# Attention of a fused transformer kernel: context keys laid in front of the tokens, and output halves joined by transposes and a sum

## The chip, the cores and the metric

The kernel runs on one core of a Trainium2 chip. The metric is device time in microseconds (us) of one execution; the runs shown are of the unchanged kernel. Engines: TensorE (PE; its weight loads are PEld), VectorE (DVE), ScalarE (ACT), GpSimd (POOL), and SyncE (SP), which issues the transfers. PSUM holds eight banks of 512 fp32 columns by 128 partitions; here three tensors S of two banks and two tensors M of one bank.

## The reference, cut to what matters

The program computes two transformer blocks over 1024 tokens of width 1024. The first has an attention with two kinds of heads, both of width 64, and 256 context keys that every query sees beside its local ones; the second block (a gated linear attention) and both feed-forward parts are not touched. What is computed in the attention:

```python
# kind a: 8 query heads, 2 key heads, window of 128 to either side, one sink per head
s_loc = einsum('bnqkgd,bnjkd->bnkgqj', qb, kb) * scale      # up to 384 local keys
s_loc = where(mask, s_loc, -inf)
s_ctx = einsum('bnqkgd,bjkd->bnkgqj', qb, k_ctx) * scale    # 256 context keys
p = softmax(concatenate([s_loc, s_ctx, sink_col], -1), -1)
o = einsum('bnkgqj,bnjkd->bnqkgd', p_loc, vb) + einsum('bnkgqj,bjkd->bnqkgd', p_ctx, v_ctx)
# kind b: 8 heads, 2-D neighbourhood of 8 x 16 positions, bias by offset, no sink
s_loc = einsum('bnqhd,bnjhd->bnhqj', qb, kg) * scale + bias # 512 or 576 local keys
...
```

Softmax is over the concatenation, so the order of the keys is free as long as scores and values agree.

## The kernel before, in words

All five engines run their own straight program, written out by Python loops; the order on each is that of the code, and signals (semaphores) tie them. The phases are: the input norm and the product with the input weights, in 18 units (`UNITS`, kinds k, q and v), attention, output product, feed-forward, second block, feed-forward. In each product, fp32 values are split into a high and a low fp32r part, and three of the four part products are summed.

A k unit gives 128 rows (two heads of 64) by 1280 columns: before, columns 0 to 1023 are tokens and 1024 to 1279 context keys, in `ka`, `kb`, and in their split copies `kh` and `kl`. TensorE has the token part in an S tensor and the context part in an M tensor; VectorE takes both out (`unit_take`), ScalarE and TensorE form the norm (`unit_norm`, `unit_sums`), and the a keys are rotated (`unit_rope`).

Attention is one software pipeline over 128 items `ITEMS`: 16 heads, 8 blocks of 128 queries each, the first 64 of kind a, the last 64 of kind b. L is the number of local keys: 256 or 384 for a, 512 or 576 for b. In iteration i the engines do, in this order:

- TensorE: `join(i-4)` (L520, L521), `scores(i)` (L551, L552, and the mask products L554 of kind a), `turn_weights(i-1)` (L567, a transpose for each 128 keys), `weigh(i-2)` (L583).
- VectorE: `take_out(i-4)` (L1317), the minimum of the negated scores (L1341 and L1345 for a; L1347 and L1351 with the bias for b), the low part of the weights of item i-1 (L1362); in every second iteration of the b part also half a row of the modulation product (L1373).
- ScalarE: the high part of the weights of item i-1 (L928), exp of item i (L935), the copy `ot` of the weighed values of item i-2 (L941).
- GpSimd: the division by the sums, and the split of the next head's queries, keys and values; SyncE moves their halves to the other partitions.

Scores of item i lie in `S[i % 2]`, columns 0 to 255 + L, at most 832; the joined output of item i lies in the same S tensor at columns 960 to 1023. `ot` has 128 partitions (64 dimensions of v's high part, then 64 of its low part) and 256 columns (128 queries by the weights' high part, then by their low part). The join multiplies both column halves with `ii`, an identity stacked twice, in plain fp32, so that queries come to lie on partitions and all four parts are summed in PSUM; in the trace each such product is two instructions (x2). VectorE then copies 64 columns out. It does this after the scores of item i+4, which TensorE issues behind the join into the same S tensor:

```python
e.wait_ge(*scored(i + 4))
e.tensor_copy((oa if kind == "a" else ob)[:, b, 64 * h:64 * h + 64], S[i % 2][:, 960:1024])
```

Scores are written as column pieces, each a product with `kh` and one with `kl`: context (256 columns), first 256 tokens, the rest.

Of the kernel before, what the change touches and what calls it, by code (L numbers as in the profile page):

```python
# [13 lines left out]
KB = 1024  # L14
# [182 lines left out]
def build(nc, T, out):  # L197
    o = 16512

    def at(name, off, shape, dt):  # L200
        return nc.alloc_sbuf_tensor_at(name, shape, dt, offset=off)
# [57 lines left out]
    osq = at("osq", AH + 37 * KB, [128, 512], F)  # L259
    ii = at("ii", AH + 39 * KB, [128, 64], F)  # L260
    ot = at("ot", AH + 61 * KB, [128, 2, 256], F)
# [35 lines left out]
    def flat(x):  # L297
        return x.rearrange("p a b -> p (a b)")

    def vo_part(m):  # L300
# [4 lines left out]
    with ExitStack() as ctx:  # L305
# [39 lines left out]

        SL, ML, BANK = Slots(3), Slots(2), {}

        def unit_tile(u):
# [7 lines left out]
        def tensor_program(e):  # L356
# [82 lines left out]
            def unit_sums(u):  # L439
# [15 lines left out]
                e.wait_ge(*a_sq(u))  # L455
                e.matmul(S[j][:, 0:512], blk, sq[:, 0:512], start=True, stop=True)
                i = e.matmul(S[j][:, 512:1024], blk, sq[:, 512:1024], start=True, stop=True)
                if kind == "k":
                    i = e.matmul(M[jc][:, 0:256], blk, sq[:, 1024:1280], start=True, stop=True)
                i.then_inc(*summed.mark(u))  # L460

            def unit_rope(u):
                kind, m, rope = UNITS[u]
                if not rope:
                    return
                dst = ka[:, :] if kind == "k" else qa[:, m, :]
# [48 lines left out]
            def join(i):  # L515
                s = i % 2
                e.wait_ge(*a_ot(i))
                if i == 0:
                    e.wait_ge(*d_set("ii"))
                e.matmul(S[s][:, 960:1024], ot[:, i % 2, 0:128], ii[:, :], start=True, stop=False)  # L520
                e.matmul(S[s][:, 960:1024], ot[:, i % 2, 128:256], ii[:, :], start=False, stop=True).then_inc(*joined.mark(i))  # L521

            def scores(i):
# [17 lines left out]
                D, Q = S[s], qs[:, z, 128 * b:128 * b + 128]  # L541
                w, n1 = 256 + L, min(256, L)
                parts = [(0, 256, 1024, None)]
                if kind == "a":
                    parts.append((256, 256 + n1, k0, (256, mlb) if b > 0 else (384, mrb)))
                    if L > 256:
                        parts.append((512, w, k0 + 256, (512, mrb)))
                else:
                    parts += [(256, 512, k0, None), (512, w, k0 + 256, None)]
                for c0, c1, kc, m in parts:  # L550
                    e.matmul(D[:, c0:c1], Q, kh[:, z, kc:kc + c1 - c0], start=True, stop=False)  # L551
                    i_ = e.matmul(D[:, c0:c1], Q, kl[:, z, kc:kc + c1 - c0], start=False, stop=m is None)  # L552
                    if m is not None:
                        i_ = e.matmul(D[:, m[0]:m[0] + 128], idb[:, :], m[1][:, :], start=False, stop=True)  # L554
# [235 lines left out]
        def scalar_program(e):  # L790
# [44 lines left out]
            def unit_norm(u):  # L835
                kind, m, rope = UNITS[u]
                j = SL.of["sum", u]
                if kind == "v":
# [4 lines left out]
                    return  # L843
                dst, w = unit_tile(u)
                e.wait_ge(*d_ev(u))
                if u > 0:
# [6 lines left out]
                if u > 0:  # L853
                    e.wait_ge(*d_nrm(max(v for v in range(u) if UNITS[v][0] != "v")))
                i = e.activation(rs[:, 0:1024], S[j][:, :], ACT.Ln, bias=EPS)
                i.then_inc(*a_ln.mark(u))
                last = u
                if kind == "k":
                    last = ("c", u)
                    e.activation(rs[:, 1024:1280], M[ML.of["sum", u]][:, 0:256], ACT.Ln, bias=EPS).then_inc(*a_ln.mark(last))  # L860
                e.wait_ge(*a_ln(last))
# [337 lines left out]
        def vector_program(e):  # L1199
# [46 lines left out]
            def unit_take(u):  # L1246
# [10 lines left out]
                else:  # L1257
                    d = unit_tile(u)[0]
                if kind != "q":
                    e.tensor_copy(d[:, 1024:1280], M[ML.of[u]][:, 0:256]).then_inc(*d_ev.mark(("c", u)))  # L1260
                e.tensor_copy(d[:, 0:1024], S[SL.of[u]][:, :]).then_inc(*d_ev.mark(u))

# [38 lines left out]
            e.wait_ge(*summed(NU - 1))  # L1301
            e.tensor_tensor(ii[:, :], cst[:, C_ID:C_ID + 64], cst[:, C_ID + 64:C_ID + 128], ALU.add).then_inc(*d_set.mark("ii"))
            e.memset(pp[:, :, 832:896], 0.0).then_inc(*d_set.mark("pad"))
# [7 lines left out]
            def take_out(i):  # L1311
# [267 lines left out]
        def gpsimd_program(e):  # L1579
# [20 lines left out]
            def unit_rope(u):  # L1600
                kind, m, rope = UNITS[u]
                if not rope:
                    return
                x = unit_tile(u)[0][:, 0:1024]
                e.wait_ge(*roped(u))
# [458 lines left out]
```

## Time and profile before

| | |
|---|---|
| median of 3 runs | 2894.28 us (2889.22 to 2894.30) |
| profiled execution | 2890.93 us, its span 2889.1 us |
| mean granted TensorE clock | 0.975 of full speed |
| busy share of the span | TensorE 94%, its weight loads 77%, VectorE 34%, ScalarE 34%, GpSimd 32% |
| attention: L1317, first and last start | 404.3 and 769.6 us |

The shares are those of the whole span; most of it is long products, in which TensorE alone sets the pace. In the attention stage the other engines have much higher shares, so it is read by itself. In a row of the timeline the first number is the start, the second the duration; where a row merges several instructions the duration is from the first start to the last end, and a bracket says how long the engine had been idle and what ended that.

### The profile page before, as it was taken

The page shows a single profiled execution, that of the slowest core. Times are in us where ns is not written, and L with a number is a line of the kernel's source. Part 1 is how long each engine was busy: PE and PEld are TensorE (multiplying, and loading weights), DVE is VectorE, ACT ScalarE, POOL GpSimd, SP SyncE. Part 2 cuts the span into 40 slices and gives each one's busy share as a digit, 9 for nine tenths or more (in the row PEclk, how much of TensorE's full clock was granted, in tenths as well). Part 3 has the DMA queues.
Part 4 walks back from the last instruction along what each step waited for, and adds up shares of the span by engine and source line. Part 5 has one row for each costly group of instructions (what it writes and reads, how often), then busy time and mean ns, then how long its engine had stood idle before and what let it go on. Part 6 is the DMA issues. An engine that isn't in the chain of part 4 may idle for free.

```text
span 2889.1 us, 32346 instructions
## 1 busy us (share of the span) xinstructions
PE 2725.0 (94%) x13256; PEld 2217.6 (77%) x13256; DVE 992.3 (34%) x1389; ACT 978.9 (34%) x1422; POOL 938.6 (32%) x466
## 2 busy tenths in 40 slices
PE   4899989988798999999999899999999999999996
PEld 3677769888786888888888577767768888888885
DVE  6411258888713211112112411122334223232323
ACT  2433468777724111111111442134233222222233
POOL 4211325455233322232323511112543233232224
PEclk7999989999999999999999999999999999999998
DMA  7001032233211111111111311000211111211111
GB/s 264 22 30 37 8 102 67 81 107 109 108 45 37 43 53 49 47 48 48 48 55 34 113 37 37 29 23 30 102 40 45 47 52 39 63 31 62 48 37 73
DMA packets 50708, 169.54 MB, mean 59 GB/s; under 512 B 6129, under 2 KB 6257, under 8 KB 50434
## 3 DMA queue, kind: packets, MB, share of 16 engines
q1 hardware_dynamic: 50562, 167.47, 18.2%
q8 instruction: 107, 1.75, 0.2%
q14 instruction: 39, 0.32, 0.0%
HBM read 148.31 MB, written 8.39 MB: 54 GB/s over the span
## 4 chain that ended last, share of the span: by engine, by line
PE 84%; DVE 7%; issue 4%; ACT 3%; POOL 1%; DMA 1%; SPq 0%; DVEq 0%; ACTq 0%; POOLq 0%
PE S L364 27%; PE S L365 27%; PE S L665 15%; PE S L567 2%; PE M L583 2%; DVE tt__105 L1407 2%; PE M L734 1%; PE M L367 1%; PE S L551 1%; DVE mjk L1213 1%; PE S L552 1%; PE S L749 1%; PE S L513 1%; DVE nmx L1341 1%; ACT pp L935 1%
## 5 line engine op out<-in xcount | busy, mean ns | idle before, releaser
L1587 POOL TENSOR_TENSOR wl<-raw,wh 128x1024 fp32r<-128x1024 f32 (+2 forms) x227 | 469.0, 2067 | 1420.1 <-ACT wh L801 1420.1
L801 ACT ACTIVATE wh<-raw 128x1024 fp32r<-128x1024 f32 (+2 forms) x227 | 209.7, 924 | 1335.7 <-PE S L365 886.1
L364 PE MATMUL S<-hh,wh 128*128 128x512 f32 (+1 forms) x1176 | 479.1, 407 | 61.8 <-DVE hcl L1243 27.5
L364 PE MATMUL S<-hl,wh 128*128 128x512 f32 (+1 forms) x1176 | 460.4, 391 | 4.8 <-POOL hl L1706 3.4
L365 PE MATMUL S<-hh,wh 128*128 128x512 f32 (+1 forms) x1176 | 461.4, 392 | 0.0
L365 PE MATMUL S<-hh,wl 128*128 128x512 f32 (+1 forms) x1176 | 461.2, 392 | 0.0
L364 PE MATMUL S<-hh,wl 128*128 128x512 f32 (+1 forms) x1176 | 461.1, 392 | 0.0
L365 PE MATMUL S<-hl,wh 128*128 128x512 f32 (+1 forms) x1176 | 460.4, 392 | 0.0
L364 PEld LDWEIGHTS S<-hh,wh 128*128 128x128 f32 (+1 forms) x1176 | 221.6, 188 | 123.4 <-issue 67.1
L364 PEld LDWEIGHTS S<-hl,wh 128*128 128x128 f32 (+1 forms) x1176 | 221.0, 188 | 58.5 <-POOL hl L1706 8.1
L364 PEld LDWEIGHTS S<-hh,wl 128*128 128x128 f32 (+1 forms) x1176 | 221.4, 188 | 48.7 <-issue 0.6
L365 PEld LDWEIGHTS S<-hh,wl 128*128 128x128 f32 (+1 forms) x1176 | 221.4, 188 | 45.0 <-issue 0.6
L365 PEld LDWEIGHTS S<-hh,wh 128*128 128x128 f32 (+1 forms) x1176 | 221.9, 189 | 43.2 <-issue 4.1
L365 PEld LDWEIGHTS S<-hl,wh 128*128 128x128 f32 (+1 forms) x1176 | 220.9, 188 | 43.8 <-issue 0.3
L665 PE MATMUL S<-fh,wh 128*128 128x512 f32 x704 | 217.9, 391 | 4.3 <-DVE fh L1441 3.4
L665 PE MATMUL S<-fl,wh 128*128 128x512 f32 x704 | 217.8, 391 | 0.6 <-POOL fl L1725 0.6
L665 PE MATMUL S<-fh,wl 128*128 128x512 f32 x704 | 217.6, 390 | 0.0
L1457 DVE TENSOR_TENSOR pr<-sg,S 128x1024 f32<-128x1024 f32 x22 | 26.9, 1222 | 394.4 <-PE S L365 381.3
L665 PEld LDWEIGHTS S<-fh,wh 128*128 128x128 f32 x704 | 132.4, 189 | 32.9 <-DVE fh L1441 3.8
L665 PEld LDWEIGHTS S<-fl,wh 128*128 128x128 f32 x704 | 132.5, 188 | 29.2 <-POOL fl L1725 1.7
L665 PEld LDWEIGHTS S<-fh,wl 128*128 128x128 f32 x704 | 132.7, 189 | 27.6
L1396 DVE SCALAR_TENSOR_TENSOR xt<-S,mv,xt 128x1024 f32<-128x1024 f32 (+1 forms) x50 | 61.9, 1241 | 245.3 <-PE S L665 181.1
(275 smaller groups left out, 3763.4 us busy)
## 6 DMA issues: line engine op xcount, KB each, us to landing
mr<-in_w_modT SPq DMA_DIRECT2D x32, 512.0 KB, 3.6
raw<-in_w_d SPq DMA_DIRECT2D x48, 256.0 KB, 2.7
raw<-in_w_f1g SPq DMA_DIRECT2D x22, 512.0 KB, 3.5
raw<-in_w_f1u SPq DMA_DIRECT2D x22, 512.0 KB, 3.4
raw<-in_w_f2g SPq DMA_DIRECT2D x22, 512.0 KB, 3.4
raw<-in_w_f2u SPq DMA_DIRECT2D x22, 512.0 KB, 3.4
raw<-in_w_d SPq DMA_DIRECT2D x32, 320.0 KB, 2.9
raw<-in_w_in SPq DMA_DIRECT2D x18, 512.0 KB, 3.5
```

The source lines that it names most:

```text
L364: e.matmul(S[j][0:mm, 0:512], lhs, x[:, k, 0:512], start=first, stop=last)
L365: i = e.matmul(S[j][0:mm, 512:1024], lhs, x[:, k, 512:1024], start=first, stop=last)
L367: i = e.matmul(M[jc][0:mm, 0:256], lhs, cx[n // 2][:, k, :], start=first, stop=last)
L513: e.matmul(bank[k], idb[:, :], mlb[:, :].unsqueeze(1).to_broadcast([128, 4, 128]), start=True, stop=True)
L551: e.matmul(D[:, c0:c1], Q, kh[:, z, kc:kc + c1 - c0], start=True, stop=False)
L567: i_ = e.transpose(bank[k][:, 128 * (x - 4 * half):128 * (x - 4 * half) + 128], pp[:, i % 3, 128 * x:128 * x + 128], ID)
L583: i_ = e.matmul(M[i % 2][:, 0:256], vh[:, n % 2, v, :], pt[:, i % 2, :, x, :], start=x == 0, stop=x == nt - 1)
L665: i = e.matmul(S[j][:, r], wt[:, w % 2, k, :], x[:, q, r], start=first, stop=last)
L801: e.activation(flat(wh[:, w % 2, :, :])[:, 0:n], raw[:, (w + NPM) % 3, 0:n], ACT.Copy).then_inc(*w_hi.mark(w))
L1396: i = e.scalar_tensor_tensor(x, S[j][:, r], gate, x, ALU.mult, ALU.add)
L1407: e.scalar_tensor_tensor(tt_[:, TT[tag, k], :], xt[:, k, :], gain[:, k:k + 1], rs2[:, :], ALU.mult, ALU.mult).then_inc(*d_y.mark((tag, k)))
L1587: e.tensor_tensor(l, raw[:, (w + NPM) % 3, 0:n], h.bitcast(F), ALU.subtract).then_inc(*w_lo.mark(w))
```

## The change

Two edits, and what follows from them.

Keys: the 256 context columns now stand first in `ka`, `kb`, `kh` and `kl`, tokens at 256 to 1279 (`unit_cols` says where). The context and the first 256 local keys, which need not be neighbours, are read by one product of 512 columns whose moving operand has two pieces (`two_blocks`). Values keep their order.

Output: the join's two fp32 products become two transposes into columns 832 to 959 (both value parts for the weights' high part) and 960 to 1023 (the value's high part for the weights' low part, 64 partitions in). The three blocks of 64 columns are added by VectorE as it takes them out; the product of the two low parts is no longer in the sum. `ii` and the operation that made it go.

```diff
+    def two_blocks(x, step, n):
+        return bass.AP(tensor=x.tensor, offset=x.offset, ap=[list(x.ap[0]), [step, 2], [1, n]])
...
+        def unit_cols(u):
+            kind = UNITS[u][0]
+            if kind == "q":
+                return slice(0, 1024), None
+            return (slice(256, 1280), slice(0, 256)) if kind == "k" else (slice(0, 1024), slice(1024, 1280))
...
             def join(i):
                 s = i % 2
                 e.wait_ge(*a_ot(i))
-                if i == 0:
-                    e.wait_ge(*d_set("ii"))
-                e.matmul(S[s][:, 960:1024], ot[:, i % 2, 0:128], ii[:, :], start=True, stop=False)
-                e.matmul(S[s][:, 960:1024], ot[:, i % 2, 128:256], ii[:, :], start=False, stop=True).then_inc(*joined.mark(i))
+                e.transpose(S[s][:, 832:960], ot[:, s, 0:128], ID)
+                e.transpose(S[s][:, 960:1024], ot[0:64, s, 128:256], ID[0:64, 0:64]).then_inc(*joined.mark(i))
...
-                w, n1 = 256 + L, min(256, L)
-                parts = [(0, 256, 1024, None)]
+                w = 256 + L
+                masks = []
                 if kind == "a":
-                    parts.append((256, 256 + n1, k0, (256, mlb) if b > 0 else (384, mrb)))
+                    masks.append((256, mlb) if b > 0 else (384, mrb))
                     if L > 256:
-                        parts.append((512, w, k0 + 256, (512, mrb)))
-                else:
-                    parts += [(256, 512, k0, None), (512, w, k0 + 256, None)]
-                for c0, c1, kc, m in parts:
-                    e.matmul(D[:, c0:c1], Q, kh[:, z, kc:kc + c1 - c0], start=True, stop=False)
-                    i_ = e.matmul(D[:, c0:c1], Q, kl[:, z, kc:kc + c1 - c0], start=False, stop=m is None)
+                        masks.append((512, mrb))
+                for c0, c1 in ((0, 512), (512, w)):
+                    if c0 == c1:
+                        continue
+                    m = next((m for m in masks if c0 <= m[0] < c1), None)
+                    for x in (kh, kl):
+                        keys = x[:, z, 0:256] if c0 == 0 else x[:, z, k0 + 512:k0 + w]
+                        if c0 == 0:
+                            keys = two_blocks(keys, 256 + k0, 256)
+                        i_ = e.matmul(D[:, c0:c1], Q, keys, start=x is kh, stop=x is kl and m is None)
                     if m is not None:
                         i_ = e.matmul(D[:, m[0]:m[0] + 128], idb[:, :], m[1][:, :], start=False, stop=True)
...
-            e.tensor_tensor(ii[:, :], cst[:, C_ID:C_ID + 64], cst[:, C_ID + 64:C_ID + 128], ALU.add).then_inc(*d_set.mark("ii"))
...
-                e.tensor_copy((oa if kind == "a" else ob)[:, b, 64 * h:64 * h + 64], S[i % 2][:, 960:1024]).then_inc(*d_out.mark(i))
+                e.tensor_reduce((oa if kind == "a" else ob)[:, b, 64 * h:64 * h + 64],
+                                S[i % 2][:, 832:1024].rearrange("p (a c) -> p c a", c=64), AX, ALU.add).then_inc(*d_out.mark(i))
```

The other lines of the diff put `unit_cols` in place of fixed columns in the k units (take-out, sums, norm, rotation); their operations keep sizes and order.

TensorE, one iteration with an a item of 384 local keys: join, scores with both masks, transposes, weighing. Names are output<-moving,stationary. Before:

```order
L520 MATMUL S<-ii,ot 128x64
L521 MATMUL S<-ii,ot 128x64
L551 MATMUL S<-kh,qs 128x256
L552 MATMUL S<-kl,qs 128x256
L551 MATMUL S<-kh,qs 128x256
L552 MATMUL S<-kl,qs 128x256
L554 MATMUL S<-mlb,idb 128x128
L551 MATMUL S<-kh,qs 128x128
L552 MATMUL S<-kl,qs 128x128
L554 MATMUL S<-mrb,idb 128x128
L567 MATMUL S<-cst,pp 128x128 x5
L583 MATMUL M<-pt,vh 128x256 x5
```

After, the same iteration:

```order
L529 MATMUL S<-cst,ot 128x128
L530 MATMUL S<-cst,ot 128x64
L565 MATMUL S<-kh,qs 128x512
L565 MATMUL S<-kl,qs 128x512
L567 MATMUL S<-mlb,idb 128x128
L565 MATMUL S<-kh,qs 128x128
L565 MATMUL S<-kl,qs 128x128
L567 MATMUL S<-mrb,idb 128x128
L580 MATMUL S<-cst,pp 128x128 x5
L596 MATMUL M<-pt,vh 128x256 x5
```

The join stays two rows, now with the identity (`cst`) as moving operand, and four score products of 256 columns are two of 512. In a b item the third pair (256 or 320 columns) stays as it is; the order of the four steps is the same in both.

VectorE, an a iteration, with what each instruction waits for in brackets. Before:

```order
L1317 COPY oa<-S 128x64 [waits scored]
L1341 TENSOR_REDUCE nmx<-S 128x1 [waits scored]
L1345 TENSOR_SCALAR nmx<-nmx,snk 128x1 [waits d_nm]
L1362 TENSOR_TENSOR pt<-S,pt 128x512 [waits a_pt]
L1362 TENSOR_TENSOR pt<-S,pt 128x128 [waits a_pt]
```

After:

```order
L1331 TENSOR_REDUCE oa<-S 128x64 [waits scored]
L1356 TENSOR_REDUCE nmx<-S 128x1 [waits scored]
L1360 TENSOR_SCALAR nmx<-nmx,snk 128x1 [waits d_nm]
L1377 TENSOR_TENSOR pt<-S,pt 128x512 [waits a_pt]
L1377 TENSOR_TENSOR pt<-S,pt 128x128 [waits a_pt]
```

Nothing moves: the take-out stands at the same place, with the same wait, as a reduction.

## Rows read from the trace of the kernel before

**Rows 1.** Windows: stretch, us; PE, PEld, DVE, ACT, POOL busy (x); PEclk, DMA, GB/s.
```profile
483.68:503.67 19.99, 19.54 (x166) 18.57 (x166) 16.08 (x43) 16.70 (x46) 9.34 (x7) 1.00 0.22 68
729.27:752.67 23.40, 22.44 (x187) 21.31 (x185) 21.30 (x61) 18.75 (x41) 1.23 (x2) 1.00 0.08 24
```

**Rows 2.** Timeline: start us, us, engine line op, xcount; two a items, all engines.
```profile
498.80 0.23 DVE L1317 COPY oa<-S 128x64 f32<-128x64 f32 x1 [0.45 <-PE S L554]
...
500.04 0.80 ACT L935 ACTIVATE pp<-S,nmx 128x640 f32<-128x640 f32 x1
...
501.00 0.75 PE L567 MATMUL S<-cst,pp 128*128 128x128 f32 x5
...
501.50 0.84 PE L583 MATMUL M<-pt,vh 128*128 128x256 f32 x5
...
502.18 0.33 PE L520 MATMUL S<-ii,ot 128*128 128x64 f32 x2
...
502.54 0.36 PE L551 MATMUL S<-kh,qs 128*128 128x256 f32 x1
...
502.74 0.28 PE L552 MATMUL S<-kl,qs 128*128 128x256 f32 x1
...
503.40 0.23 PE L554 MATMUL S<-mrb,idb 128*128 128x128 bf16 x1
...
503.67 0.23 DVE L1317 COPY oa<-S 128x64 f32<-128x64 f32 x1
```

**Rows 3.** Timeline: an input product, TensorE with 512 columns.
```profile
1100.63 0.39 PE L364 MATMUL S<-hh,wh 128*128 128x512 f32 x1
...
1101.54 0.39 PE L364 MATMUL S<-hl,wh 128*128 128x512 f32 x1
```

**Rows 4.** Timeline, TensorE: scores straight behind weighing, before the first join.
```profile
398.31 0.72 PE L583 MATMUL M<-pt,vh 128*128 128x256 f32 x4
398.86 0.28 PE L551 MATMUL S<-kh,qs 128*128 128x256 f32 x1
398.98 0.28 PE L552 MATMUL S<-kl,qs 128*128 128x256 f32 x1
```

**Rows 5.** Groups by line and form, VectorE, attention stage.
```profile
L1341 DVE TENSOR_REDUCE nmx<-S 128x1 f32<-128x640 f32 x45 | 36.6, 813 | 0.0
L1347 DVE TENSOR_REDUCE nmx<-S 128x1 f32<-128x256 f32 x64 | 26.2, 410 | 0.0
L1317 DVE COPY ob<-S 128x64 f32<-128x64 f32 x64 | 14.1, 220 | 12.2 <-PE S L552 8.6 <-PE S L521 3.3
```

**Rows 6.** Timeline, VectorE: a pair of b items, from copy to copy.
```profile
729.27 0.22 DVE L1317 COPY ob<-S 128x64 f32<-128x64 f32 x1
729.41 0.42 DVE L1347 TENSOR_REDUCE nmx<-S 128x1 f32<-128x256 f32 x1
...
731.92 0.23 DVE L1317 COPY ob<-S 128x64 f32<-128x64 f32 x1 [0.17 <-PE S L552]
...
734.93 0.22 DVE L1317 COPY ob<-S 128x64 f32<-128x64 f32 x1
```

**Rows 7.** Waits of the attention stage: us in total, times, longest.
```profile
PEld S L567 <- ACT pp L935: 38.9, 56, 2.5
PE S L567 <- ACT pp L935: 26.8, 27, 2.3
```

**Rows 8.** Windows of Rows 1's columns: two stalls and what follows each.
```profile
616.00:620.00 4.00, 2.06 (x18) 1.80 (x16) 3.96 (x10) 1.73 (x4) 3.72 (x3) 1.00 0.58 123
620.00:624.00 4.00, 3.81 (x20) 3.81 (x21) 3.17 (x9) 2.71 (x8) 2.15 (x2) 0.57 0.01 2
696.00:700.00 4.00, 2.10 (x18) 1.84 (x16) 3.96 (x9) 1.75 (x4) 3.74 (x3) 1.00 0.59 127
700.00:704.00 4.00, 3.78 (x33) 3.78 (x34) 3.80 (x12) 3.02 (x9) 2.16 (x2) 1.00 0.00 0
```

**Rows 9.** Timeline, VectorE, ahead of the attention stage.
```profile
370.13 0.22 DVE L1302 TENSOR_TENSOR ii<-cst 128x64 f32<-128x64 f32 x1
```

More of the change, by code:

```diff
@@ L259, in build @@
     osq = at("osq", AH + 37 * KB, [128, 512], F)
-    ii = at("ii", AH + 39 * KB, [128, 64], F)
     ot = at("ot", AH + 61 * KB, [128, 2, 256], F)
@@ L455, in unit_sums @@
                 e.wait_ge(*a_sq(u))
-                e.matmul(S[j][:, 0:512], blk, sq[:, 0:512], start=True, stop=True)
-                i = e.matmul(S[j][:, 512:1024], blk, sq[:, 512:1024], start=True, stop=True)
+                t0 = unit_cols(u)[0].start
+                e.matmul(S[j][:, 0:512], blk, sq[:, t0:t0 + 512], start=True, stop=True)
+                i = e.matmul(S[j][:, 512:1024], blk, sq[:, t0 + 512:t0 + 1024], start=True, stop=True)
                 if kind == "k":
-                    i = e.matmul(M[jc][:, 0:256], blk, sq[:, 1024:1280], start=True, stop=True)
+                    i = e.matmul(M[jc][:, 0:256], blk, sq[:, 0:256], start=True, stop=True)
                 i.then_inc(*summed.mark(u))
@@ L465, in unit_rope @@
                     return
-                dst = ka[:, :] if kind == "k" else qa[:, m, :]
+                dst = unit_tile(u)[0][:, unit_cols(u)[0]]
                 j = SL.take(e, ("rope", u), (d_rp, u))
@@ L844, in unit_norm @@
                 dst, w = unit_tile(u)
+                t, x = unit_cols(u)
                 e.wait_ge(*d_ev(u))
@@ L854, in unit_norm @@
                     e.wait_ge(*d_nrm(max(v for v in range(u) if UNITS[v][0] != "v")))
-                i = e.activation(rs[:, 0:1024], S[j][:, :], ACT.Ln, bias=EPS)
+                i = e.activation(rs[:, t], S[j][:, :], ACT.Ln, bias=EPS)
                 i.then_inc(*a_ln.mark(u))
@@ L859, in unit_norm @@
                     last = ("c", u)
-                    e.activation(rs[:, 1024:1280], M[ML.of["sum", u]][:, 0:256], ACT.Ln, bias=EPS).then_inc(*a_ln.mark(last))
+                    e.activation(rs[:, x], M[ML.of["sum", u]][:, 0:256], ACT.Ln, bias=EPS).then_inc(*a_ln.mark(last))
                 e.wait_ge(*a_ln(last))
@@ L1258, in unit_take @@
                     d = unit_tile(u)[0]
+                t, x = unit_cols(u)
                 if kind != "q":
-                    e.tensor_copy(d[:, 1024:1280], M[ML.of[u]][:, 0:256]).then_inc(*d_ev.mark(("c", u)))
-                e.tensor_copy(d[:, 0:1024], S[SL.of[u]][:, :]).then_inc(*d_ev.mark(u))
+                    e.tensor_copy(d[:, x], M[ML.of[u]][:, 0:256]).then_inc(*d_ev.mark(("c", u)))
+                e.tensor_copy(d[:, t], S[SL.of[u]][:, :]).then_inc(*d_ev.mark(u))
             def unit_norm(u):
@@ L1603, in unit_rope @@
                     return
-                x = unit_tile(u)[0][:, 0:1024]
+                x = unit_tile(u)[0][:, unit_cols(u)[0]]
                 e.wait_ge(*roped(u))
```

## The prediction

> **What bounds the kernel now.** I read the windows first, then the timeline of the attention stage, then its waits. Attention runs from about 404 to 770 us; everything that the change touches on a repeated path lies there. It works through 128 items: 64 of kind a (local window), then 64 of kind b (neighbourhood). Over one a head, 8 items in 19.99 us or 2.50 us each, TensorE is busy 19.54 us and VectorE 16.08; over one b head, 23.40 us or 2.93 us each, TensorE 22.44 and VectorE 21.30 [rows 1]. A busy TensorE is not yet the bound: its matmuls overlap and their ends are modelled. The reader should look for starts that wait.
>
> The timeline of two a items shows a loop [rows 2]. The copy that takes an old output out of PSUM (L1317) starts at 498.80, having waited 0.45 us for TensorE's last score product. Then come the minimum, exp at 500.04, the five transposes at 501.00, the five weighing products at 501.50, the join at 502.18, the scores of the item after next at 502.54, their last product at 503.40, and the same copy again at 503.67. That is 4.87 us for two items, 2.44 each, close to the measured 2.50. So an a item is set by a ring that goes once through VectorE's take and minimum, through ScalarE's exp and through one round of TensorE. Of this ring the change shortens the TensorE part and lengthens the VectorE part.
>
> A pair of b items goes from copy to copy, 729.27, 731.92, 734.93: 5.66 us, in which VectorE idles only 0.17 us [rows 6]. Every second b item carries half a row of the modulation product (L1373) on VectorE, so there VectorE itself is within 3% of the bound. The waits agree: TensorE's transposes wait 38.9 us (weight loads) and 26.8 us (products) in all for exp [rows 7]. TensorE is not what everybody waits for.
>
> **The change, part by part.**
>
> *Scores.* Context and first 256 tokens were two products of 256 columns for each of high and low keys; now it is one of 512. A 256-column product steps on after 0.12 us (398.86 to 398.98) [rows 4]. Four of 512 columns take 1100.63 to 1101.54, 0.91 us, or 0.228 each [rows 3]. Per item 4 x 0.12 = 0.48 becomes 2 x 0.228 = 0.455: 0.025 us saved. Half of the instructions go and almost none of the time, because the columns stay. The two-piece address of the moving keys is in no row; I take 0, bounds -0.05 and +0.1 us a product, since 256-wide blocks are long against any turn between them. Laying the keys' columns the other way round costs nothing: the same copies, logarithms and products of the same sizes stand in the same places.
>
> *Join.* Before, the join takes 502.18 to 502.54, 0.36 us, and the first score product behind it steps after 0.20 us instead of 0.12 [rows 2, 4]. After, two transposes. Five transposes step from 501.00 to 501.50, 0.10 us each [rows 2], so 0.20 us; the second has 64 columns, which I count as a full one (below 0.06, above the 0.18 of a join product pair). The extra 0.08 us I keep, since the weighing products show about as much behind the transposes: 0.68 us for five against 5 x 0.12 [rows 2]. Saved: 0.16 us. Together TensorE gives 0.185 us per item, 128 x 0.185 = 23.7 us in all.
>
> *Take-out.* A copy of 64 columns becomes a sum over three strided blocks, 192 elements read. Reductions of 640 and 256 elements take 813 and 410 ns: 1.05 ns an element [rows 5]. For 192 that gives 410 - 64 x 1.05 = 343 ns against 220 for the copy, so d = 0.12 us more per item, on VectorE, ahead of the minimum that exp waits for. Nothing hides it there. No row shows a reduction with 64 results or a stride. Bounds: d = 0 if the reduction costs what the copy does, d = 0.45 if it were as long as the reduction of 512 elements would be by the same slope (0.67 us). I take 0.12, by the nearest width.
>
> *Waits.* None is added. The join still waits for ScalarE's ot, and the scores queue behind it as now. The take-out still waits for the scores of four items later, not for the join; so a quicker join helps it only through the scores. The product with the folded identity needed one VectorE operation of 0.22 us (L1302) ahead of the stage [rows 9]; it goes: -0.2 us, with TensorE's warm-up products waiting behind it.
>
> *The sum on the two rings.* In a, the ring for two items loses 0.185 and gains d = 0.12: -0.065, so 64 items give 32 x -0.065 = -2.1 us. In b, VectorE needs 5.66 - 0.17 = 5.49 us for a pair; with 2 x 0.12 more it is 5.73 against 5.66 now: +0.07, and 32 pairs give +2.2 us. TensorE's saving finds nobody waiting there. About eight long stalls, at most of the head changes from the seventh head on, are of the kind in which VectorE's chain alone runs and TensorE is busy for 2.06 or 2.10 us in 4 (two of them are in [rows 8]); each takes d more: +1.0. Sum: -2.1 + 2.2 + 1.0 - 0.2 = +0.9 us. For any d it is (32d - 5.9) + (64d - 5.4) + 8d - 0.2 = 104d - 11.5.
>
> The profiled execution took 2890.93 us (span 2889.1), the median of the runs 2894.28, 3.35 above. On the profile's own time the forecast is 2891.8; on the median's, 2895. The difference that a measurement of this kernel can tell is about 0.2%, 5.8 us.
>
> **Rivals.**
>
> *TensorE is the bound after all (faster).* Its busy time in an a head is 98% [rows 1], which speaks for it. Then all of 23.7 us comes back: 2894.3 - 23.7 = 2871. Against it stand the 0.45 us that VectorE waits inside a ring that closes at 4.87 us, and VectorE's 0.17 us of idle time in a b pair.
>
> *The strided sum is slow (slower).* The place is L1317's successor. If each element costs twice the 1.05 ns, 0.20 us come on top, d = 0.32, and the formula gives 104 x 0.32 - 11.5 = +21.8: 2916. It decides from d = 0.17 on, where the sum passes 5.8 us. For it: the three elements that it adds lie 64 apart, which no group of rows has. Against it: the two reductions that are shown follow one straight line. The Trainium skill (PSUM — Partial Sum Buffer, Specifications) says that PSUM's lines are 8 bytes and that any non-contiguous pattern slows matmuls significantly; whether that holds for VectorE's reads it does not say, and no run here shows it.
>
> *The clock falls more often (slower).* After the stall in 616 to 620 us the granted clock is 0.57 in the next 4 us and TensorE starts 20 instructions; after a nearly equal stall, 696 to 700, it stays at 1.00 and 33 start [rows 8]. A fall to the 1.2 GHz level thus costs 13 of 33 starts, 1.6 us. TensorE was busy for 2.06 and 2.10 us before it, so nearly equal stalls end either way, and a change of TensorE's work can turn more of them. Three more falls are +4.7 us and with the forecast 2900; ten more, 2912. The Trainium skill (TensorE: Matmul & The Clock Gate, PE-mode transpose) says that transposes do not count as busy in the way that matmuls do; this change turns real products into transposes. Against that rule, in an a head a fifth of TensorE's time (0.50 of 2.44 us) is transposes and the clock is 1.00 throughout [rows 1, 2]; by the rule the falls would become more, without it they stay as they are.
>
> *The change does less than it says.* If a transpose of this tile steps like a join product (0.18 for two), TensorE saves only 0.025 us an item and the a term turns to 32 x (0.12 - 0.025) = +3.0: 2900.
>
> **How the numbers follow.** Forecast, within 2889 to 2901: 0.50. TensorE-bound: 0.12. Slow strided sum: 0.14. Clock: 0.10. Small join saving: 0.05. The remaining 0.09 is a reduction nearly as short as the copy (d below 0.055, where the formula passes -5.8 us), down to 2883. Faster by over 0.2%: 0.12 + 0.08 = 0.20. Slower: 0.14 + 0.05 of the clock + 0.03 of the small saving + 0.08 of the forecast's upper edge = 0.30. The same: 0.50. The range 2884 to 2912 leaves out the first rival and the upper part of the slow sum, about 0.2.
>
> **What would show it.** In the changed profile: two transposes and then the 512-column product within 0.20 us; 512-column score products at 0.23 us steps; the sum at about 0.34 us in the groups by line; an a head at 19.7 us and a b pair at 5.7 with VectorE idle near nothing. The forecast is wrong if the sum is below 0.28 or above 0.39 us, if an a head takes under 19 us, or if windows with a clock below 1.00 in the b heads number clearly more than now.

## The result, and the profile after

| | before | after |
|---|---|---|
| median of 7 runs | 2889.97 us | 2901.04 us (2899.82 to 2902.90) |
| profiled execution, span | 2889.1 us | 2900.0 us |
| mean granted TensorE clock | 0.975 | 0.974 |
| first take-out of the attention stage | 404.26 us | 406.15 us |
| a stage: first take-out of a to first of b | 166.85 us | 170.64 us |
| b stage: first take-out of b to the last | 198.46 us | 203.99 us |

The changed kernel is slower: the ratio is 1.0034, with a 95% interval from 1.0022 to 1.0046. This is 9.8 us, and surely more than nothing. The median lies in the predicted range of 2884 to 2912 us, 6 us above the forecast of 2895. That flatters it, since the median before fell as well when more runs were taken, from 2894.28 to 2889.97 us: as a difference, +0.9 us was forecast and about +10 came. The likeliest case said "within 0.2%", and the result is outside that.

The last three rows of the table account for the 10.9 us of span: 1.9 ahead of the stage, 3.8 in a, 5.5 in b, and -0.3 behind. The 1.9 us are not put down to the change: 1.7 of them arise in the input products at 112 to 116 us, where the granted clock differs, and the changed kernel with the copy (join_copy, below) has no such fall there. These two windows, of before and then of after, have the columns of [rows 1]:

```profile
112.00:116.00 4.00, 3.82 (x14) 2.62 (x15) 0.00 (x0) 2.71 (x4) 1.30 (x1) 1.00 0.37 121
```

```profile
112.00:116.00 4.00, 3.64 (x7) 1.84 (x7) 0.00 (x0) 1.50 (x2) 1.48 (x1) 0.58 0.36 119
```

After, TensorE starts 7 products there and not 14. Among the eleven kernels of this study, before and after included, the first take-out starts between 402.8 and 406.3 us, with no tie to what each does in the attention. So 9.3 us in the attention are to be explained, where +1.1 was forecast.

The same a head and b head as in [rows 1], in the changed kernel:

```profile
487.41:507.88 20.47, 20.02 (x134) 15.31 (x134) 17.00 (x42) 16.71 (x46) 9.37 (x7) 1.00 0.21 66
739.78:763.65 23.87, 22.87 (x155) 19.18 (x153) 22.36 (x59) 18.79 (x41) 1.23 (x2) 1.00 0.07 23
```

The heads are longer by 0.48 and 0.47 us. TensorE has 32 instructions fewer in each and yet is busy 0.48 and 0.43 us longer. VectorE is busy 0.92 and 1.06 us longer. The clock stays at 1.00, so it is no reason here.

The timeline of two a items, to be laid beside [rows 2]:

```profile
502.80 0.36 DVE L1331 TENSOR_REDUCE oa<-S 128x64 f32<-128x192 f32 x1 [0.41 <-PE S L567]
503.07 0.81 DVE L1356 TENSOR_REDUCE nmx<-S 128x1 f32<-128x640 f32 x1
...
505.19 0.71 PE L580 MATMUL S<-cst,pp 128*128 128x128 f32 x5
...
505.66 0.84 PE L596 MATMUL M<-pt,vh 128*128 128x256 f32 x5
...
506.33 0.28 PE L529 MATMUL S<-cst,ot 128*128 128x128 f32 x1
...
506.54 0.27 PE L530 MATMUL S<-cst,ot 64*128 64x64 f32 x1
...
506.74 0.50 PE L565 MATMUL S<-kh,qs 128*128 128x512 f32 x1
...
507.08 0.40 PE L565 MATMUL S<-kl,qs 128*128 128x512 f32 x1
...
507.62 0.23 PE L567 MATMUL S<-mrb,idb 128*128 128x128 bf16 x1
507.88 0.36 DVE L1331 TENSOR_REDUCE oa<-S 128x64 f32<-128x192 f32 x1
```

The ring is still there and closes after 5.08 us instead of 4.87. Read the starts. The take-out holds VectorE for 0.27 us before the minimum starts (503.07 less 502.80); before it was 0.14 in the b rows [rows 6]. That is +0.13. On TensorE, from the join's start to the last masked product, [rows 2] have 502.18 to 503.40, 1.22 us; now it is 506.33 to 507.62, 1.29 us. That is +0.07, where -0.185 was forecast. The two together are +0.20, and this ring grew by 0.21. It is one pair, and of the eight overlapping pairs of this head the one that grew most: over all eight the growth is -0.01 to 0.21 us, 0.11 in the mean. So the match is in part luck. But the join's own times are steady: in the second to the sixth head the median from its start to the last masked product is 1.22 us before and 1.28 after, and the join itself 0.36 and 0.41. So the step that went wrong is already visible: the join. The first transpose starts at 506.33, the second 0.21 us later, and the first score product 0.20 us behind that: 0.41 us for the join, against 0.36 before and 0.20 in the forecast. The five transposes of the weights, which all have full size, step on in 0.094 us each (505.19 to 505.66) in the same trace.

What holds the small transpose back shows on TensorE's queue of weight loads. First the timeline of the join before the one above, whose two transposes start at 503.84 and 504.04, then the group by line and form of the whole attention stage:

```profile
503.74 0.14 PEld L529 LDWEIGHTS S<-cst,ot 128*128 128x128 f32 x1
504.04 0.14 PEld L530 LDWEIGHTS S<-cst,ot 64*128 64x128 f32 x1 [0.16 <-issue]
504.24 0.19 PEld L565 LDWEIGHTS S<-kh,qs 128*128 128x128 f32 x1
```

```profile
L529 PEld LDWEIGHTS S<-cst,ot 128*128 128x128 f32 x128 | 18.0, 141 | 1.7 <-issue 1.7
L530 PEld LDWEIGHTS S<-cst,ot 64*128 64x128 f32 x128 | 17.6, 138 | 21.7 <-issue 21.6
```

The full load of L529 starts at 503.74, 0.10 us before its product. The load of 64 partitions starts at 504.04, at the very moment of its product, after 0.16 us in which the load queue did nothing. That is no accident of one item: 21.6 us of idle time over 128 items, 0.17 us each, released by nothing that the profile shows. The load itself is not slow, 138 ns against 141.

Two rows of the kernel before bear on this. The first is a load of the second block, with 64 partitions too, for a product with 256 moving columns that is no transpose (64 products of two instructions each). The second is a load of the old join, with all 128 partitions and only 64 moving columns:

```profile
L734 PEld LDWEIGHTS M<-vo,gd 64*128 64x128 f32 x128 | 18.8, 184 | 23.2 <-issue 22.1 <-DVE gst L1504 1.1
L521 PEld LDWEIGHTS S<-ii,ot 128*128 128x128 f32 x254 | 39.3, 195 | 0.0
```

The first idles 23.2 us, 0.36 us for each of 64 products, and the full load behind it (L749) is held up by 0.33 us; the other full loads of that stage (L364, L365) idle 0.05 us each at most. The load of L521 never idles. So the wait goes with the 64 partitions, and not with transposes or with few moving columns.

VectorE in a pair of b items, beside [rows 6]:

```profile
739.78 0.35 DVE L1331 TENSOR_REDUCE ob<-S 128x64 f32<-128x192 f32 x1
740.05 0.41 DVE L1362 TENSOR_REDUCE nmx<-S 128x1 f32<-128x256 f32 x1
...
742.48 0.36 DVE L1331 TENSOR_REDUCE ob<-S 128x64 f32<-128x192 f32 x1
...
745.62 0.35 DVE L1331 TENSOR_REDUCE ob<-S 128x64 f32<-128x192 f32 x1
```

A pair takes 5.84 us (5.66 before, 5.73 forecast). The groups by line and form give the sum, which answers to the copy in [rows 5]:

```profile
L1331 DVE TENSOR_REDUCE oa<-S 128x64 f32<-128x192 f32 x64 | 22.8, 356 | 13.4 <-PE S L567 11.8
L1331 DVE TENSOR_REDUCE ob<-S 128x64 f32<-128x192 f32 x64 | 22.6, 353 | 12.1 <-PE S L565 8.3 <-PE S L530 2.9
```

It takes 355 ns, where 343 were expected. And it waits: 12.1 us in b, as long as the copy did, where VectorE was to have next to no idle time left. The waits for exp are what they were in [rows 7]:

```profile
PEld S L580 <- ACT pp L949: 40.9, 64, 2.6
PE S L580 <- ACT pp L949: 26.1, 21, 2.4
```

### The profile page after: what moved, and what is told of

Read it like the earlier page. It is cut to its first block, busy times and chain, and to the rows that moved or that the text cites. A ratio compares the mean times of both kernels' runs of the same rounds, so it can differ in the third digit from the quotient of the medians.

```text
span 2900.0 us, 31321 instructions
## 1 busy us (share of the span) xinstructions
PE 2736.1 (94%) x12744; PEld 2174.8 (75%) x12744; DVE 1007.9 (35%) x1388; ACT 979.5 (34%) x1422; POOL 938.9 (32%) x466
## 4 chain that ended last, share of the span: by engine, by line
PE 83%; DVE 7%; issue 4%; ACT 3%; POOL 1%; DMA 1%; SPq 0%; DVEq 0%; ACTq 0%; POOLq 0%
PE S L374 27%; PE S L375 27%; PE S L678 15%; PE S L565 2%; PE S L580 2%; PE M L596 2%; DVE tt__104 L1422 2%; PE M L747 1%; PE M L377 1%; DVE mjk L1227 1%; PE S L762 1%; PE S L524 1%; DVE nmx L1356 1%; DVE S L1366 1%; DMA mtl<-in_w_modT 1%
```

## The experiments

Each was timed against the kernel before on the same chip. "a head" is the time from take-out to take-out over 8 items, of the second to the sixth head, which agree within 0.1 us; "b head" is the last full one (head 14), free of the long stalls. The ratio has its 95% interval in brackets. The stages are those of the first table.

| kernel | a head | b head | a stage | b stage | ratio |
|---|---|---|---|---|---|
| before | 19.98 | 23.40 | 166.85 | 198.46 | |
| after | 20.45 | 23.87 | 170.64 | 203.99 | 1.0034 (1.0022, 1.0046) |
| keys_only | 19.96 | 23.35 | 166.75 | 200.00 | 0.9998 (0.9990, 1.0007) |
| join_only | 20.48 | 23.92 | 170.86 | 204.32 | 1.0035 (1.0022, 1.0048) |
| join_copy | 20.09 | 23.60 | 167.75 | 200.80 | 1.0005 (0.9996, 1.0014) |
| full_second | 19.78 | 23.88 | 165.41 | 202.55 | 1.0022 (1.0013, 1.0031) |
| full_over | 19.77 | 23.14 | 166.15 | 198.85 | 0.9994 (0.9985, 1.0003) |

**The keys alone.** The kernel before with the new layout of the keys and the score products of 512 columns; the join and the copy stay.

```diff
-                parts = [(0, 256, 1024, None)]
+                masks = []
...
+                for c0, c1 in ((0, 512), (512, w)):
...
+                            keys = two_blocks(keys, 256 + k0, 256)
...
```

> The key layout and the 512-column score products alone, with the old join and copy. Theory (the loss is in the join and the take-out): score products step 0.12 + 0.12 as 0.23, TensorE's score time changes by 0.02 us an item at most, an a head stays at 19.9 to 20.1 us and the time within 3 us of before. Rival (the long products or their two-piece address lose): the first 512-column product takes 0.1 us more than its columns, an a head is 20.3 us or more and the time 4 us or more above before.

Measured: 2891.99 us beside 2891.79 of before, ratio 0.9998. In its timeline, a join as before and then the new scores:

```profile
503.38 0.39 PE L533 MATMUL S<-ii,ot 128*128 128x64 f32 x2
503.57 0.47 PE L568 MATMUL S<-kh,qs 128*128 128x512 f32 x1
503.88 0.40 PE L568 MATMUL S<-kl,qs 128*128 128x512 f32 x1
504.12 0.23 PE L570 MATMUL S<-mlb,idb 128*128 128x128 bf16 x1
```

The two products take 0.31 + 0.24 = 0.55 us, hardly less than the four before (a step of 0.20 behind the join and three of 0.12: 0.56). The moving address of two pieces costs nothing, and two instructions fewer an item bring nothing. This half of the change is worth zero within 0.1%; the forecast gave it 0.025 us an item on TensorE, 3.2 us in all at the most.

Its b stage is 1.5 us longer than before with the same b head. Its trace has one more fall of the clock there (five against four), without a single added transpose. So stage sums differ by that much from one profile to the next, and the heads free of stalls are the better measure.

**The join alone.** The two transposes and the sum, on the old keys and scores.

```diff
-                e.matmul(S[s][:, 960:1024], ot[:, i % 2, 0:128], ii[:, :], start=True, stop=False)
-                e.matmul(S[s][:, 960:1024], ot[:, i % 2, 128:256], ii[:, :], start=False, stop=True).then_inc(*joined.mark(i))
+                e.transpose(S[s][:, 832:960], ot[:, s, 0:128], ID)
+                e.transpose(S[s][:, 960:1024], ot[0:64, s, 128:256], ID[0:64, 0:64]).then_inc(*joined.mark(i))
...
```

> The transposes and the sum alone, on the old key layout and 256-column products. Theory: all of the loss is here, an a head at 20.4 to 20.5 us and the time 7 to 11 us above before. Rival (the score products carry it): an a head at 20.1 or less and the time within 4 us of before.

Measured: 2903.11 us, ratio 1.0035. The whole loss is in this half: a head, b head and both stages are those of the changed kernel within 0.4 us. The transposes start at 500.86 and 501.06 and the first score product, one of 256 columns, at 501.26. So the slow join has nothing to do with the wide product behind it:

```profile
501.06 0.27 PE L518 MATMUL S<-cst,ot 64*128 64x64 f32 x1
501.26 0.39 PE L548 MATMUL S<-kh,qs 128*128 128x256 f32 x1
```

**The sum taken away.** The changed kernel, whose take-out is again a copy of 64 columns.

```diff
-                e.tensor_reduce((oa if kind == "a" else ob)[:, b, 64 * h:64 * h + 64],
-                                S[i % 2][:, 832:1024].rearrange("p (a c) -> p c a", c=64), AX, ALU.add).then_inc(*d_out.mark(i))
+                e.tensor_copy((oa if kind == "a" else ob)[:, b, 64 * h:64 * h + 64], S[i % 2][:, 832:896]).then_inc(*d_out.mark(i))
```

> The changed kernel with a copy of one 64-column block in place of the sum; it leaves out the addition of the other two blocks. Theory (the 0.13 us that the sum takes more on VectorE is the larger part of the loss, since it lies on the ring of the a items and fills VectorE in the b items): an a head falls by 4 x 0.13 to 19.9 us, a b head by 0.5 us or more, the time is 6 to 9 us below the changed kernel. Rival (TensorE's join, 0.40 us instead of 0.36, is the loss): an a head at 20.3 or more, the time at most 3 us below the changed kernel.

Measured: 2893.54 us, ratio 1.0005. Against the changed kernel's 2901.04 the sum costs 7.5 us, within the 6 to 9 expected (8.4 by the two ratios, 6.1 by the stages of the traces). But the a head stops at 20.09 and does not come down to 19.9: with a copy that costs what the old one did, this kernel is still 0.11 us a head above before, and 0.20 in the b head. A quicker join would have put it below. That was the first sign that the other term was wrong.

**Second transpose at full size, in a.** The columns of S that an a item leaves free allow two transposes of 128 x 128 there.

```diff
+                if ITEMS[i][1] == "a":
+                    e.transpose(S[s][:, 704:832], ot[:, s, 0:128], ID)
+                    e.transpose(S[s][:, 832:960], ot[:, s, 128:256], ID).then_inc(*joined.mark(i))
+                    return
...
+                x0 = 704 if kind == "a" else 832
...
```

The scores of the first b items reach over column 704, in front of the take-out of the last a items, whose results are therefore wrong; the counts and the order of the work stay.

> The changed kernel with the second transpose of the a items over all 128 partitions and 128 columns (its last 64 columns are not read); b items as changed. Theory (the second transpose's 64-partition operand keeps its weight load from overlapping its neighbours): from first to second transpose 0.10 instead of 0.20 us, from the second to the scores 0.2 or less, join together 0.30 or less, an a head 0.4 us or more shorter than 20.46. Rival (the 0.20 us steps come from turning from fp32r products to fp32 transposes and back, whatever the shape): both steps stay at 0.20 us and an a head at 20.4 or more.

Measured: 2897.64 us, ratio 1.0022. The a head falls from 20.45 to 19.78 and the b head stays (23.88). In the timeline:

```profile
503.46 0.27 PE L530 MATMUL S<-cst,ot 128*128 128x128 f32 x1
503.57 0.27 PE L531 MATMUL S<-cst,ot 128*128 128x128 f32 x1
503.60 0.48 PE L569 MATMUL S<-kh,qs 128*128 128x512 f32 x1
```

A second transpose over twice the partitions and twice the columns makes the join 0.14 us long instead of 0.41. It isn't the transpose as such, nor the switch from transposes to products. Partitions and moving columns change together here; the rows of L734 and L521 above say that the partitions decide.

**Both transposes at full size, in all items.** The low part's transpose comes first, and the high part's is laid over its unwanted half, so the same three blocks of 64 columns are summed from the same columns.

```diff
-                e.transpose(S[s][:, 832:960], ot[:, s, 0:128], ID)
-                e.transpose(S[s][:, 960:1024], ot[0:64, s, 128:256], ID[0:64, 0:64]).then_inc(*joined.mark(i))
+                e.transpose(S[s][:, 832:960], ot[:, s, 128:256], ID)
+                e.transpose(S[s][:, 896:1024], ot[:, s, 0:128], ID).then_inc(*joined.mark(i))
```

> The changed kernel with both transposes over 128 partitions and 128 columns in all items: first the one of the weights' low part into columns 832 to 959, then the one of the high part into 896 to 1023, over the half that isn't wanted. Theory (the 64-partition operand cost the saving): the join takes 0.14 to 0.25 us instead of 0.40, an a head 19.7 to 19.9 us; b heads stay near the changed kernel's 23.9 (the one without GpSimd's loads), as VectorE sets them; time 2892 to 2897. Rival (in b items TensorE matters as well): that b head falls below 23.5 and the time below 2891.

Measured: 2890.26 us beside 2891.80, ratio 0.9994: the loss is gone, with the sum still in place, and the time is below the 2892 to 2897 expected. Timeline of the products, then of their loads, then the groups:

```profile
501.58 0.28 PE L529 MATMUL S<-cst,ot 128*128 128x128 f32 x1
501.70 0.27 PE L530 MATMUL S<-cst,ot 128*128 128x128 f32 x1
501.72 0.48 PE L565 MATMUL S<-kh,qs 128*128 128x512 f32 x1
502.04 0.40 PE L565 MATMUL S<-kl,qs 128*128 128x512 f32 x1
```

```profile
501.48 0.14 PEld L529 LDWEIGHTS S<-cst,ot 128*128 128x128 f32 x1
501.58 0.14 PEld L530 LDWEIGHTS S<-cst,ot 128*128 128x128 f32 x1
501.70 0.19 PEld L565 LDWEIGHTS S<-kh,qs 128*128 128x128 f32 x1
```

```profile
L1331 DVE TENSOR_REDUCE ob<-S 128x64 f32<-128x192 f32 x64 | 22.5, 351 | 7.0 <-PE S L565 4.2 <-PE S L530 2.8
L530 PEld LDWEIGHTS S<-cst,ot 128*128 128x128 f32 x127 | 18.1, 143 | 0.0
```

The load of L530 now starts 0.12 us before its product and is never idle. And the b head falls to 23.14: a faster TensorE does help in b, which the forecast had denied and the rival of this experiment had said. VectorE's wait ahead of the take-out went from 12.1 to 7.0 us, so a good part of that wait had been for TensorE.

**The sum's stride.** The changed kernel with a sum over three neighbouring elements instead of three that lie 64 apart.

```diff
-                                S[i % 2][:, 832:1024].rearrange("p (a c) -> p c a", c=64), AX, ALU.add).then_inc(*d_out.mark(i))
+                                S[i % 2][:, 832:1024].rearrange("p (c a) -> p c a", c=64), AX, ALU.add).then_inc(*d_out.mark(i))
```

> The changed kernel with its sum over three neighbouring elements instead of three that lie 64 apart; same counts, another result. Theory (VectorE reads PSUM at the same pace along any pattern): the sum stays at 350 to 360 ns and the time within 3 us of the changed kernel. Rival (the stride costs): it falls by 30 ns or more, and the time by 3 us or more.

Measured: 2901.99 us, ratio 1.0035, as the changed kernel. In its groups:

```profile
L1331 DVE TENSOR_REDUCE ob<-S 128x64 f32<-128x192 f32 x64 | 22.7, 354 | 11.8 <-PE S L565 7.9 <-PE S L530 3.1
```

With the stride 353 ns, without it 354: VectorE's read of PSUM pays nothing for it.

**What the stalls are.** The kernel before, where only the half rows of the modulation product (L1373) are moved, from every second item to the last four items of each head.

```diff
-                if i >= 56 and i % 2 and i < 128:
-                    n, half = i // 4, i // 2 % 2
+                if i >= 56 and i % 8 >= 4 and i < 128:
+                    n, half = 2 * (i // 8) + i % 8 // 2 - 2, i % 2
...
-                    if i == 57:
+                    if i == 60:
...
```

> The kernel before, with the half rows of the modulation product on VectorE (one in each second item from item 56 on) moved to the last four items of each head, when GpSimd has split the next head's keys. Theory (the long waits at head changes come from this product waiting for GpSimd's 2.4 to 2.9 us operations, and the clock falls follow them): the 5.2 us periods become 3.0 or less, hardly any window below a clock of 1.00 between 570 and 760 us, time 12 to 20 us below before. Rival (VectorE is the bound and only its work counts): the time within 4 us of before.

Measured: 2877.57 us, ratio 0.9952 (0.9939 to 0.9964), a gain of 14 us. The stall of 616 us in [rows 8] is, in the kernel before, this:

```profile
614.18 2.93 POOL L1645 TENSOR_TENSOR kl<-kb,kh 64x1280 fp32r<-64x1280 f32 x1
614.94 2.73 DVE L1373 CUSTOM_DVE_ANT_0 mr<-mr,cb 128x512 f32<-128x512 f32 x1
```

```profile
734.32 0.68 DVE L1373 CUSTOM_DVE_ANT_0 mr<-mr,cb 128x512 f32<-128x512 f32 x1
```

The same VectorE operation takes 0.68 us alone and 2.73 us when it starts while GpSimd prepares the keys' low part. It ends 0.56 us after GpSimd does (614.94 + 2.73 = 617.67 against 614.18 + 2.93 = 617.11), so it seems to do nearly all of its work only then. The kernel before has eight such long operations, and so has the changed one. In all sixteen GpSimd is subtracting (`kl` or `qx`) and started first, by 0.01 to 1.63 us, and VectorE ends 0.55 to 0.56 us behind it. Where VectorE started first, at 557.09, GpSimd's subtraction grew instead, to 2.71 us from 2.38. The Trainium skill (SBUF — State Buffer, SBUF: two separate sides) says that a VectorE operation with two SBUF inputs and a GpSimd operation that reads SBUF exclude each other, and that the second waits for the whole of the first. The trace agrees, with 2.73 us against 0.68. With the half rows elsewhere, head 11 has no stall; windows of before and of mr_late:

```profile
651.22:678.10 26.88, 23.77 (x186) 22.81 (x185) 23.48 (x59) 18.75 (x41) 14.64 (x10) 0.94 0.36 103
```

```profile
640.53:664.07 23.54, 22.49 (x186) 21.34 (x185) 21.17 (x58) 18.75 (x41) 14.23 (x11) 1.00 0.41 117
```

The b heads 10 to 12 and 14 take 23.54 us each where before they took 26.60, 26.88, 25.18 and 23.40. Heads 8, 9 and 13 keep stalls (26.64, 25.69, 26.45). In 8 and 13 a half row still meets a subtraction of GpSimd (`qx`, at 576.19 and 698.88), and takes 2.91 and 2.92 us; in 9 ScalarE loads two tables of 1.28 us each, at 594.14 and 595.75, and TensorE idles. The clock's falls go with the stalls: 0.94 against 1.00 in the same head, and in all of the attention two falls instead of five, each about 5 us after the start of one of the two long half rows that are left. The expectation had hardly any fall and no long period left, so it was right in the gain and too hopeful there.

**Both cures together.** full_over with the half rows moved.

```diff
-                if i >= 56 and i % 2 and i < 128:
+                if i >= 56 and i % 8 >= 4 and i < 128:
...
```

> Both of them together: full-size transposes with the sum, and the modulation product moved. Theory: the gains add less VectorE's 0.13 us per b item: a head 19.8 us, time 0 to 5 us above the moved product alone. Rival (without the stalls TensorE is the later engine in b): the time 2 us or more below the moved product alone.

Measured: 2877.87 us, ratio 0.9951 (0.9937 to 0.9964), the same as mr_late within the intervals. Its a head is 19.78, but its b head is 23.73, where full_over had 23.14: four half rows in a row, on a VectorE that carries the sum as well, seem to take back what the quick join gave. That is read from the heads alone and was not tried by itself.

**A version faster than before and after.** The keys of the changed kernel, its sum with two full transposes in a, the old products and the copy in b, and the half rows moved.

```diff
+                if ITEMS[i][1] == "b":
+                    if ITEMS[i - 1][1] == "a":
+                        e.wait_ge(*d_set("ii"))
+                    e.matmul(S[s][:, 960:1024], ot[:, s, 0:128], ii[:, :], start=True, stop=False)
+                    e.matmul(S[s][:, 960:1024], ot[:, s, 128:256], ii[:, :], start=False, stop=True).then_inc(*joined.mark(i))
+                    return
+                e.transpose(S[s][:, 832:960], ot[:, s, 128:256], ID)
+                e.transpose(S[s][:, 896:1024], ot[:, s, 0:128], ID).then_inc(*joined.mark(i))
...
```

> Each stage with what suits it: a items join by two full-size transposes and the sum, b items by the old two products and the copy, and the modulation product moved behind GpSimd's key split. Theory (a is set by a ring that full transposes shorten by 0.2 us a head, b by VectorE, which the copy spares 0.13 us an item): a head 19.8, b head 23.5 us, time 1 to 3 us below the moved product alone, 14 to 18 below before. Rival (the two stages' savings are within what the clock's falls move): the time within 1 us of the moved product alone, or above.

Measured: 2876.45 us (2875.01 to 2878.48), ratio 0.9949 (0.9935 to 0.9962). Its a head is 19.77 and its b head 23.51. It beats before by 14.7 us and the changed kernel by some 25 us. Against mr_late it is 1.1 us, less than the intervals can tell apart: nearly all of its gain is the moved half rows, not the join.

## Why the prediction was right or wrong

**The scores: right.** The forecast kept the columns and saved 0.025 us an item. keys_only shows no change (0.9998), and 0.55 against 0.56 us for the products: 0.01 us saved. The two-piece address costs nothing, as assumed.

**The join: wrong, and this is the step that failed.** It is the TensorE term of the sum, a saving of 0.16 us an item. The prediction said of the two transposes: "so 0.20 us; the second has 64 columns, which I count as a full one (below 0.06, above the 0.18 of a join product pair)". It measured 0.40 to 0.41, above what the upper bound allowed (0.10 + 0.18). The bounds were about columns, and what decided was the other side of the operand: the stationary block has 64 of 128 partitions. The prediction looked at no load of such a shape, though the trace of before has them in its second block (L734), each product with 0.36 us of idle load queue. The load of the small transpose doesn't run ahead beside the transpose before it, and the score product behind it comes late as well. The saving of 0.16 us is in truth a loss of 0.05. With full blocks the join takes 0.14, better than forecast, and then the time comes out near the forecast too: full_over is 1.5 us below before, not clear of noise, where +0.9 was said. From the changed kernel to full_over it is 10.8 us. The Trainium skill (TensorE: Matmul & The Clock Gate, LDWEIGHTS) says that a load's time goes by its columns and not by its rows. Of the load itself the trace says the same, 138 against 141 ns; what it costs is where the load may start. That page's section "Step-by-step: what each phase is for" says that loads are pulled ahead of products where the row groups don't conflict or where they go to the background buffer. This leaves room for what is seen; which of its conditions fails here, no run shows. The mechanism behind the late load stays open.

**The take-out: right.** d was to be 0.12 us; it is 0.13 (0.27 against 0.14 before the next operation starts), and the sum's 355 ns are 12 more than the line through two reductions gave. join_copy puts its price at 7.5 us.

**The ring in a: right in shape, too steep in size.** The ring shown measured 5.08 us, which is 4.87 plus the two changes, but over a head the pairs of items grew by 0.12 us, not by 0.20. Taking the kernels pairwise gives what one item passes on: the sum (after less join_copy) 0.36 us a head or 0.045 an item for 0.13 us of VectorE; the short transposes (after less full_over) 0.68 us a head or 0.085 an item for 0.28 us of TensorE (1.29 less the 1.00 of full_over, 501.58 to 502.58). Each is a third, where the ring of two items says a half. What takes up the rest was not sought. These shares are differences of kernels; none has the quick join without the sum, so that the two add up is assumed.

**b bound by VectorE: wrong.** The forecast let VectorE's d through in full there and TensorE's saving not at all, because VectorE idled only 0.17 us in a pair [rows 6]. Measured in the b head: the sum 0.27 us or 0.034 an item for 0.13, and the join 0.73 us or 0.091 an item for 0.28. So b passes on a quarter and a third, nearly as a does. The pair in [rows 6] was a poor sample: over all b items VectorE waited 12.2 us at the copy alone [rows 5], 0.38 a pair, mostly for TensorE's scores. That row was in the prediction's own groups and should have settled it, and [rows 1] says the same: in the b head VectorE is busy 21.30 of 23.40 us, so it idles 0.53 us a pair.

**The stalls: right about the chain and the count, the term not shown.** VectorE's chain alone runs there, mr_late shows why, and the long operations are eight, as said. These are as long after as before (2.73 us for that of [rows 8] and its successor). The term of +1.0 can't be told from the scatter of the stalled heads, which move by 1 us and more from kernel to kernel.

**The sum of the parts.** With the measured join and d in the prediction's own scheme, a gives 32 x (0.07 + 0.13) = +6.4, b 64 x 0.13 - 5.4 = +2.9, the stalls +1.0 and `ii` -0.2: +10.1, beside the 9.8 us of the ratio. It fits partly by luck. The stages measured +3.8 and +5.5: a passes on less than the scheme says, and b more, of which about 1.5 may be one more fall of the clock, as in keys_only. Still the join is the mis-sized term that moved the total, since the same scheme with the forecast's join gives +0.9, and the case "a transpose of this tile steps like a join product" named its result, 2900 us, with a chance of only 0.05. Of what the prediction would look for, an a head of 19.7 us (20.45), a join of 0.20 us (0.41) and an idle VectorE near nothing in b (12.1 us of waits) all failed; but its three signs of being wrong were about the sum, an a head under 19 us and the clock, and none of them would catch a slow join.

**The rivals.** TensorE as the bound: refuted in that form, since full_over makes TensorE's part of an a item 0.22 us shorter than before (1.00 against 1.22), which over 128 items would be some 28 us, and with 0.13 us more on VectorE it is within 0.1% or so of before. The slow strided sum: refuted by straight_sum and the 355 ns. The clock: at most a small part. In 4-us windows from 536 to 772 us the granted clock is below 0.95 in five places before and in six after; one more is 1.6 us by the prediction's price. But keys_only, with no transpose added, has six as well, and in the second to the sixth a head the clock stays at 1.00 with seven transposes an item instead of five. So nothing here speaks for the rule on transposes. (Ten falls more would be 2911 us by that price, not 2912.)

## What to carry to other kernels

Give a transpose between full-size work all 128 partitions, even if half of the result is thrown away; that paid here. Look for the shape of a new operation in the whole trace of before, not only in the stage that is changed: the second block had it. Look in the queue of weight loads whether each load starts ahead of its product, before trusting a count of columns. Where two engines are both at 80% busy or more in one stage, price a change on either at a part of its size (here about a quarter to a third) and read the waits over the whole stage, not one quiet pair of items. And when one VectorE operation has two very different durations, look what GpSimd does in the long ones; moving it gained 14 us here, and the whole rewrite of the join lost 10.

## What the runs showed of the hardware

- A transpose whose stationary block has 64 partitions, between full ones: 0.20 us to it and 0.20 from it to the next product, against 0.11 to 0.12 and 0.02 to 0.03 with 128 partitions. Its load idles 0.17 us first, as the mean of 128 items; with 128 partitions it idles 0.0 (full_over). The loads of 64 partitions in the second block idle 0.36 us ahead of each product (L734, before).
- A VectorE product of two SBUF operands took 2.73 us instead of 0.68 while GpSimd ran a subtraction of two SBUF operands that had started first. In 16 such cases it ended 0.55 to 0.56 us after GpSimd.
- A VectorE sum of 192 fp32 elements of PSUM into 64 took 353 ns with a stride of 64 elements and 354 ns without one.
- A product of 512 columns with a moving operand in two pieces of 256 is no slower than two products of 256 (two take 0.55 us, four of 256 take 0.56, keys_only and before).
